# Residual taken from the gathered rows, one weight slot more, and a tail summed on two engines

## What is computed

```python
def _hier_moe(x, ...):                      # gate: for each token, weight of each expert, two are nonzero
    for g in range(N_EXPERT_GROUPS):
        hg = jnp.einsum('nd,edf->nef', x, w_gate[g])
        hu = jnp.einsum('nd,edf->nef', x, w_up[g])
        a = jax.nn.silu(hg) * hu * gate[:, g, :, None].astype(x.dtype)
        y = y + jnp.einsum('nef,efd->nd', a, w_down[g]).astype(jnp.float32)
...
h1 = layer_norm(DN_ALPHA * x + mix, ln1_g, ln1_b)
f = _hier_moe(h1, ...)
return layer_norm(DN_ALPHA * h1 + f, ln2_g, ln2_b)        # DN_ALPHA = 2 ** 0.25
```

## Time and profile before

| | |
|---|---|
| time, median of 3 runs | 1012.26 us (1011.37 to 1013.74) |
| profiled execution: its own time | 1013.08 us |
| profiled execution: span | 1011.3 us |
| PE busy | 906.9 us, 90% |
| DVE busy | 553.9 us, 55% |
| ACT busy | 410.1 us, 41% |
| POOL busy | 135.6 us, 13% |
| DMA, mean over the span | 270 GB/s |

### The profile page before, as it was taken

The page is one execution under the profiler, slowest core; times in us unless marked ns, Lnnn a source line. Parts: engine busy times, 40 slices in busy tenths (PEclk is TensorE's granted clock), DMA queues, the critical chain, the costliest instruction groups (busy, mean ns, idle before and its releaser), DMA issues.

```text
span 1011.3 us, 13331 instructions
## 1 busy us (share of the span) xinstructions
PE 906.9 (90%) x5132; PEld 644.8 (64%) x5132; DVE 553.9 (55%) x1023; ACT 410.1 (41%) x748; POOL 135.6 (13%) x83
## 2 busy tenths in 40 slices
PE   6999999986999999769999835999999999999684
PEld 6999879953555545437888524666666666656331
DVE  5202020049566665683554367676767676767248
ACT  5202020033564555471222122646465555546145
POOL 0000000140000000000000002254545321121100
PEclk9999999998999999988999955999999999999987
DMA  9999999198686666409722291899999999997293
GB/s 350 328 346 338 375 351 348 56 391 244 215 327 236 244 235 225 167 1 359 244 89 68 77 385 48 301 358 372 358 358 352 358 354 371 361 360 274 83 381 130
DMA packets 54847, 273.49 MB, mean 270 GB/s; under 512 B 13984, under 2 KB 16544, under 8 KB 39680
## 3 DMA queue, kind: packets, MB, share of 16 engines
q1 hardware_dynamic: 46016, 247.97, 67.8%
q0 software_dynamic: 8768, 24.66, 6.9%
HBM read 256.33 MB, written 95.30 MB: 348 GB/s over the span
## 4 chain that ended last, share of the span: by engine, by line
PE 77%; DVE 11%; DMA 5%; ACT 3%; issue 3%; SPq 0%; POOLq 0%; DVEq 0%; ACTq 0%
PE psum L636 69%; PE psum L695 4%; PE psum L874 2%; DMA back<-w_gu 2%; DMA front<-w_gu 2%; DVE back L1222 1%; DVE front L1232 1%; DVE front L1233 1%; DVE front L1579 1%; ACT back L490 1%; DVE stats L1207 1%; DVE back L1204 1%; PE psum L834 1%; ACT back L986 1%; DMA middle<-pair_d 1%
## 5 line engine op out<-in xcount | busy, mean ns | idle before, releaser
L636 PE MATMUL psum<-back,front 128*64 128x128 f32 (+1 forms) x896 | 148.6, 359 | 7.7 <-ACT back L490 4.4
L1645 POOL DMA_INDIRECT pair_d<-front,back x32 | 84.1, 2628 | 200.4 <-ACT front L1097 143.2
L636 PEld LDWEIGHTS psum<-back,front 128*64 128x64 f32 (+1 forms) x896 | 70.3, 148 | 62.9 <-issue 53.7
L636 PE MATMUL psum<-gu_high,xg_high 128*112 128x512 f32 x256 | 104.3, 407 | 2.1 <-DVE xg_low L1472 2.1
L636 PE MATMUL psum<-gu_high,xg_low 128*112 128x512 f32 x256 | 102.0, 399 | 0.0
L636 PE MATMUL psum<-x_high,w_high 128*128 128x352 f32 x288 | 94.2, 327 | 8.3 <-DVE w_low L361 8.3
L636 PE MATMUL psum<-gu_low,xg_high 128*112 128x512 f32 x256 | 101.5, 397 | 0.0
L636 PE MATMUL psum<-front 64*128 64x256 f32 (+5 forms) x384 | 91.5, 494 | 10.8 <-DVE stats L1204 10.1
L636 PE MATMUL psum<-x_low,w_high 128*128 128x352 f32 x288 | 93.5, 325 | 0.0
L636 PE MATMUL psum<-x_high,w_low 128*128 128x352 f32 x288 | 93.5, 325 | 0.0
L490 ACT COPY back<-psum 128x512 f32<-128x512 f32 (+1 forms) x88 | 46.9, 547 | 85.5 <-PE psum L695 85.3
(11 more groups left out here) (199 smaller groups left out, 1626.4 us busy)
## 6 DMA issues: line engine op xcount, KB each, us to landing
out_win_k_s<-cache_win_k SPq DMA_DIRECT2D x16, 2044.0 KB, 13.7
out_win_v_s<-cache_win_v SPq DMA_DIRECT2D x16, 2044.0 KB, 12.6
back<-w_down SPq DMA_DIRECT2D x24, 1024.0 KB, 14.3
front<-w_gu SPq DMA_DIRECT2D x22, 1024.0 KB, 11.9
middle<-w_gu SPq DMA_DIRECT2D x22, 1024.0 KB
back<-w_gu SPq DMA_DIRECT2D x20, 1024.0 KB, 14.4
back<-winkT SPq DMA_DIRECT2D x8, 1792.0 KB, 7.6
back<-cache_win_v SPq DMA_DIRECT2D x8, 1024.0 KB, 7.2
```

The source lines that it names most:

```text
L636: return nc.tensor.matmul(out, lhsT, rhs, start=start, stop=stop, skip_group_check=True)
L1645: G.indirect_dma_start(pair_d, bass.IndirectOffsetOnAxis(ap=IDX[0:CAP, NE + e:NE + e + 1], axis=0), YS[e % 2][0:CAP, :], None, bounds_chec ...
```

## The change

1. Residual. ALPHA * h1 is no longer added in the tail. Each token has two expert rows, and the whole sum is scaled by 2 / ALPHA: each expert's output row becomes (2 / ALPHA) * weight * down + h1, with h1 from the gathered rows in XG. Two such rows add up to (2 / ALPHA) * (ALPHA * h1 + f). The normalisation undoes the factor: the variance is scaled by ALPHA^2 / 4, and the gain ln2_g by ALPHA / 2. XG is therefore kept until the output is written, and has five buffers. The gather of expert e + 3 no longer waits for PE's transposes of expert e.
2. Who does what in the expert stage. DVE now makes both halves of the output (y_out, each a scalar_tensor_tensor of 112 x 512 from PSUM and XG). ACT gets active_out, ahead of silu.
3. Weights. There are four w_gu slots and five w_down slots; the new ones lie where H1 lay. The first loads now include w_gu of expert 3 and w_down of expert 4, behind a wait for the last transposes and stores of H1. Then the load for e waits for the products of e - 4.
4. Tail. Chunks 0, 4 and 8 are summed by DVE in SBUF (own_sum), the other six by PE. The separate pass L1579 is gone: ACT and the first DVE pass read the sum from PSUM or from YP.

The diff, without its overflow path and renamed counts:

```diff
-        GU_AT, GUH_AT = (0, 18576, 27024), (4096, 22672)
+        GU_AT, GUH_AT = (0, 18576, 27024, 37520), (4096, 22672)
...
-        WD = [at(x, 2, D) for x in (11264, 44688, 46736, 48784)]
-        XG = [at(x, D) for x in (31120, 32144, 50832)]
+        WD = [at(x, 2, D) for x in (11264, 44688, 46736, 48784, 41616)]
+        XG = [at(x, D) for x in (31120, 32144, 50832, 35472, 36496)]
...
+        PE_SUM = [c for c in range(CH) if c % 4]
+
+        def row_sum(c):
+
+            if c % 4 == 0:
+                return YP[c][:, 0, :]
+            j = PE_SUM.index(c)
+            return PS[:, 1024 * (j % 4):1024 * (j % 4) + 1024]
+
+        def summed(eng, c):
+
+            if c % 4:
+                eng.wait_ge(s_ysum, PE_SUM.index(c) + 1)
+            else:
+                eng.wait_ge(s_vsum, c // 4 + 1)
...
             load_dn(sp, 3)
-
-            for e in range(3, NE):
+            sp.wait_ge(s_ht, 2 * CH)
+            sp.wait_ge(s_h1d, 16 * CH)
+            for half in range(2):
+                load_gu(sp, 3, half)
+            load_dn(sp, 4)
+
+            for e in range(4, NE):
                 for half in range(2):
-                    sp.wait_ge(s_gu, 2 * (e - 3) + half + 1)
+                    sp.wait_ge(s_gu, 2 * (e - 4) + half + 1)
                     load_gu(sp, e, half)
-                if e >= 4:
-                    sp.wait_ge(s_y, e - 3)
+                if e >= 5:
+                    sp.wait_ge(s_y, e - 4)
                     load_dn(sp, e)
...
             def down(e):
                 pe.wait_ge(s_at, e + 1)
-                pe.wait_ge(s_wd[e % 4], 16 * (e // 4 + 1))
-                if e:
-                    pe.wait_ge(s_ya, e)
-                    pe.wait_ge(s_yd, e)
+                pe.wait_ge(s_wd[e % 5], 16 * (e // 5 + 1))
                 for n in range(2):
+                    if e:
+                        pe.wait_ge(s_yd, 2 * (e - 1) + n + 1)
                     for f in range(2):
...
-            for c in range(CH):
+            pe.wait_ge(s_yd, 2 * NE)
+            for j, c in enumerate(PE_SUM):
                 m = rows(c)
                 pe.wait_ge(s_yp[c], 16)
-                if c >= 4:
-                    pe.wait_ge(s_f1, c - 3)
+                if j >= 4:
+                    pe.wait_ge(s_f1, PE_SUM[j - 4] + 1)
...
-            def y_half(e):
-                act.wait_ge(s_y, e + 1)
+            def active_out(e):
+                act.wait_ge(s_tt, e + 1)
                 if e >= 2:
-                    act.wait_ge(s_ys[e % 2], 16 * (e // 2))
-                nc.scalar.activation(YS[e % 2][0:CAP, 0:512], bank(4)[0:CAP, :], ACT.Copy,
-                                     scale=GS[0:CAP, e:e + 1]).then_inc(s_ya, 1)
+                    act.wait_ge(s_y, e - 1)
+                nc.scalar.copy(AT[e % 2][:, :, 0:CAP], bank(6)[:, 0:2 * P].rearrange("p (a n) -> p a n", a=2)[:, :, 0:CAP]).then_inc(s_at, 1)
...
             for e in range(NE):
+                if e:
+                    active_out(e - 1)
                 silu(e)
                 if e + 1 < NE:
                     tokens_rounded(e + 1)
                 if e + 2 < NE:
                     weights_rounded(e + 2)
-                if e:
-                    y_half(e - 1)
-            y_half(NE - 1)
+            active_out(NE - 1)
...
-                r, mu, sq, std = RF[c][0:m, :], MV2[0:m, c, 0:1], MV2[0:m, c, 1:2], MV2[0:m, c, 2:3]
-                act.wait_ge(s_f1, c + 1)
+                r, mu, sq, std = row_sum(c)[0:m, :], MV2[0:m, c, 0:1], MV2[0:m, c, 1:2], MV2[0:m, c, 2:3]
+                summed(act, c)
...
-                nc.scalar.activation(std, sq, ACT.Sqrt, scale=1.0 / D, bias=EPSC[0:m, :]).then_inc(s_std2, 1)
+                nc.scalar.activation(std, sq, ACT.Sqrt, scale=ALPHA ** 2 / 4 / D, bias=EPSC[0:m, :]).then_inc(s_std2, 1)
...
-                step(V_.scalar_tensor_tensor(r, r, mu, GB2[0:m, 0, :], ALU.add, ALU.mult))
-                V_.scalar_tensor_tensor(r, r, std, GB2[0:m, 1, :], ALU.mult, ALU.add).then_inc(s_fo, 1)
+                V_.scalar_tensor_tensor(out, r, mu, GB2[0:m, 0, :], ALU.add, ALU.mult).then_inc(s_f1, 1)
+                dve.wait_ge(s_f1, c + 1)
+                V_.scalar_tensor_tensor(out, out, std, GB2[0:m, 1, :], ALU.mult, ALU.add).then_inc(s_fo, 1)
...
-            step(V_.tensor_tensor(v1, v1, p1, ALU.mult))
+            step(V_.scalar_tensor_tensor(v1, v1, 2.0 / ALPHA, p1, ALU.mult, ALU.mult))
...
-            def y_half(e):
+            def y_out(e):
                 dve.wait_ge(s_y, e + 1)
                 if e >= 2:
                     dve.wait_ge(s_ys[e % 2], 16 * (e // 2))
-                V_.tensor_scalar(YS[e % 2][0:CAP, 512:1024], bank(5)[0:CAP, :], GS[0:CAP, e:e + 1], None, ALU.mult).then_inc(s_yd, 1)
+                for n in range(2):
+                    h = slice(512 * n, 512 * n + 512)
+                    V_.scalar_tensor_tensor(YS[e % 2][0:CAP, h], bank(4 + n)[0:CAP, :], GS[0:CAP, e:e + 1], XG[e % 5][0:CAP, h],
+                                            ALU.mult, ALU.add).then_inc(s_yd, 1)
...
-            dve.wait_ge(s_y, NE)
+            dve.wait_ge(s_gb2, 32)
+            step(V_.tensor_scalar(GB2[:, 0, :], GB2[:, 0, :], ALPHA / 2, None, ALU.mult))
+
+            def own_sum(c):
+                dve.wait_ge(s_yp[c], 16)
+                y = YP[c][0:rows(c)]
+                V_.tensor_tensor(y[:, 0, :], y[:, 0, :], y[:, 1, :], ALU.add).then_inc(s_vsum, 1)
+
+            own_sum(0)
             for c in range(CH):
-                m = rows(c)
-                dve.wait_ge(s_ysum, c + 1)
-                V_.scalar_tensor_tensor(RF[c][0:m, :], H1[0:m, c, :], ALPHA, PS[0:m, 1024 * (c % 4):1024 * (c % 4) + 1024],
-                                        ALU.mult, ALU.add).then_inc(s_f1, 1)
-                if c:
-                    normalised(c - 1)
-            normalised(CH - 1)
+                if c % 4 == 3:
+                    own_sum(c + 1)
+                normalised(c)
...
             gather(1)
-            G.memset(XG[2], 0.0).then_inc(s_zero, 1)
+            for i in range(2, 5):
+                last = G.memset(XG[i], 0.0)
+            last.then_inc(s_zero, 1)
             await_(s_zero, 2)
             gather(2)
             for e in range(NE):
                 if e + 3 < NE:
-                    await_(s_tp, 2 * e + 2)
                     gather(e + 3)
                 if e:
-                    pool.wait_ge(s_ya, e)
-                    await_(s_yd, e)
+                    await_(s_yd, 2 * e)
                     scatter(e - 1)
```

More of the change, by code:

```diff
@@ L133, in build @@
         CATH, CATL = overlay("cat_high", 8448, KT, TOK), overlay("cat_low", 18576, KT, TOK)
-        GU_AT, GUH_AT = (0, 18576, 27024), (4096, 22672)
+        GU_AT, GUH_AT = (0, 18576, 27024, 37520), (4096, 22672)
         GUH = [overlay(f"gu_high{s}", GUH_AT[s], KT, 2 * DE) for s in range(2)]
-        GUL = [overlay(f"gu_low{s}", GU_AT[s], KT, 2 * DE) for s in range(3)]
+        GUL = [overlay(f"gu_low{s}", GU_AT[s], KT, 2 * DE) for s in range(4)]
         XGH = [overlay(f"xg_high{s}", (33168, 16896)[s], KT, CAP) for s in range(2)]
@@ L467, in load_gu @@
             k = slice(4 * half, 4 * half + 4)
-            sp.dma_start(GUF[e % 3][:, k, :], I["w_gu"][e][:, k, :]).then_inc(s_gf[e % 3][half], 16)
+            sp.dma_start(GUF[e % 4][:, k, :], I["w_gu"][e][:, k, :]).then_inc(s_gf[e % 4][half], 16)
         def load_dn(sp, e):
-            sp.dma_start(WD[e % 4], I["w_down"][e]).then_inc(s_wd[e % 4], 16)
+            sp.dma_start(WD[e % 5], I["w_down"][e]).then_inc(s_wd[e % 5], 16)
         R0 = 13600 + 324
@@ L1495, in _ @@
             for e in range(NE):
-                if e:
-                    active_out(e - 1)
                 if e >= 2:
-                    y_half(e - 2)
+                    y_out(e - 2)
                 if e + 1 < NE:
@@ L1504, in _ @@
                     tokens_rest(e + 1)
-            active_out(NE - 1)
-            y_half(NE - 2)
-            y_half(NE - 1)
+            y_out(NE - 2)
+            y_out(NE - 1)
             with overflow(dve):
```

63 lines of the change are left out of this document (26 added, 37 removed).

## The result

The changed kernel takes 999.29 us in the median of 4 runs (998.31 to 1000.77); the kernel before, beside it, 1011.82 us (4 runs, 1009.55 to 1013.74). The ratio is 0.9878 with a 95% interval of 0.9853 to 0.9904. The profiled execution took 1000.77 us, its span is 998.9 us against 1011.3: 12.4 us less, where the prediction's sum was 11.1 less. The medians differ by 12.5 us.

A forecast was written before the change was run, and what follows sets the result against it. PE, 77% of the chain, was taken to bound the kernel, with late w_gu transfers behind expert 21 and DVE in the tail. -3.96 + 0.15 - 7.3 = -11.1 us gave 1001.1 us from 1012.26; range 998.4 to 1006.5.

The forecast's parts named there:

- The beat to expert 31: Expert stage: with the fourth w_gu slot the 9.97 us beat holds to expert 31, at 936.06: -3.96 us.
- The lag: Expert stage: w_gu issue to landing grows 0.64 us per expert, to 22.5 us at the last load, 6 us inside.
- The early loads at nothing: Before the first gather: 3 MB more of loads fit the empty stretch, cost 0; uncovered, at most 8.9 us.
- The swap at nothing: Expert stage: DVE makes both output halves, ACT takes active_out; cost 0, since DVE has 2.9 us spare per expert.
- End of the stage: Last down starts about 0.55 us sooner, two DVE halves in a row add 0.7: sum +0.15 us.
- The tail: After chunk 0 lands (T0): DVE ends at T0 + 36.9 against T0 + 44.2 before, -7.3 us.
- PE's first sum: Tail, chunk 1: first 8 matmuls behind a long idle stretch take 6.12 us, later sums 3.43 each.
- The rival with a fast first sum: Tail: PE's first sum is not slow, chunks 1 to 3 come 2.7 us sooner: 998.4 us; chance 0.07.
- The stage that gains nothing: Expert stage: loads lag faster than 0.64 per expert or early loads issue late: 1005.1 us; chance 0.12.
- The tail that loses its overlap: Tail: ACT and DVE wait for each other, 0.4 us for each of 8 chunks: 1004.3 us; chance 0.10.
- The late scatter: Expert stage: DVE waits for the scatter two experts back, PE behind it; at 22.0 us landing, 1025 us; chance 0.03.
- PSUM as a source: Tail: the skill's rule makes six first DVE passes 0.4 us longer in all; the forecast took PSUM and SBUF as equal.

The follow-up runs named there:

- the one with fewer bytes: The changed kernel with three w_gu and four w_down slots, odd experts from 5 on loading 64 of 1024 w_down columns (output wrong): 1000.29 us.
- the late fill: The changed kernel with all slots, but the fourth w_gu slot first filled only when expert 0's products free PE: 1001.26 us.
- the kernel with the POOL sums: The changed kernel with the pair sums of chunks 4 and 8 on POOL instead of DVE: 1001.0 us.

## Why the prediction was right, term by term

- **The beat to expert 31.** Forecast 936.06 for its start, 936.01 came. That this agrees to 0.05 us is luck in part: it needs a stage that begins where before's did (626.3), and after's began at 626.5, where other traces have 623.9 to 626.8. The term of 3.96 us came out at 4.01 by this row and the earlier trace rows, 4.2 by the stage's length. The runs with three slots show that the w_gu slot earns it, the one with fewer bytes that lag is the cause, the late fill that the deadline is near 28.7 us.
- **The lag.** Forecast 22.5 us at the end, by 0.64 us per expert; it was 24.8. From 650 to 850 it grew by 18.0 us in 20 experts, 0.9 each, then levelled out. In the seven other kernels with four slots and the early loads, the last load took 22.8 to 24.5 us, so the forecast lies just below all eight. The straight line was loose: the margin was 3.9 us and not 6. Before's lag at 770, 13.2 us, is that of a single load; the four-slot kernels that fill early have medians of 13.9 to 16.0 there, the loads of the three-slot kernels took 13.3 to 15.0. No run explains the spread. From 840 on the late rounds of before also held its loads back.
- **The early loads at nothing.** They moved from before 606 to 619, and the first gather takes 4.25 us from issue to landing (4.18 before). Zero stands. Without the cover, filled late, they cost 0.8 us and not the 8.9 that bounded it, because they no longer stand ahead of the gather.
- **The swap at nothing.** Right with four slots, as the run with the copy back on DVE shows. Not with three, where ACT's order seems to cost about 1.5 us, by one trace on each side. The prediction asked only whether active_out would be in time in a steady beat; it did not ask what it waits behind when a load is late.
- **End of the stage.** From expert 31's start to the last scatter it is 15.85 us, before 15.67: +0.18, forecast +0.15. The last down starts after 0.74 us of waiting instead of 1.23, and the two halves of the output behind it take 1.41.
- **The tail.** Forecast T0 + 36.9, measured T0 + 35.7. The forecast times ran 1.0 to 1.2 us late from the first PE sum on: 8.8 against 7.8 for its end, 14.3 against 13.4 for DVE's end of chunk 1, 17.8 against 16.8, 21.7 against 20.7. Ahead of it they agree: chunk 0's add done at 1.4 (1.3), ACT's root at 5.4 (5.4), DVE's two passes at 8.3 (8.3). So one term was mis-sized, **PE's first sum: 6.12 us taken from before, 5.07 measured**. The eleven traces that begin it idle gave 5.1 to 6.7 us, in the median 6.3, and the six other traces in which the tail is that of after end it at T0 + 36.3 to 37.3. So 6.12 was a fair value, the forecast of T0 + 36.9 is what most traces of this tail show, and the trace of after drew a quick first sum. The rival with a fast first sum put it at 3.43, which none of them came near.
- **Rivals.** The stage that gains nothing: excluded by 309.53. The tail that loses its overlap: DVE waits 2.30 us for chunk 1 and 0.63 for chunk 2, behind PE's late first sum, and from there on no gap between its passes is over 0.1 us. The late scatter: the scatters did grow, from 9.8 to 11.9 us in the median, yet the maximum moved only from 12.9 to 13.1, and PE's waits for DVE L1501 are one of 0.7 us in all, the last down. The Trainium skill, DMA: Bandwidth & Descriptors, section Issuing engines are not separate DMA queues, has all issuers share the 16 engines. The traces show no effect of the length of the w_gu backlog on the scatter: from the end of its issue to its landing the scatter takes 7.5 us in the median of 640 to 730 and 7.3 of 820 to 920, while the w_gu loads go from 5 to 25. What made it longer is its issue on POOL, which counts from the same start: 4.55 us in after for all but the last three; in before 4.25 in the first half of the stage, where it landed in 10.2 to 12.9, and 0.96 in the late rounds, where it landed in 8.1 to 8.5. Counted from the end of the issue the median is 7.2 us in before and 7.4 in after. So the 8.1 us of the earlier trace rows, which the prediction held against this rival, belonged to a short issue and said less than it seemed; the rival failed all the same.
- **PSUM as a source.** By the Trainium skill, VectorE: DVE Perf Modes, section on the TRN2 errata, the tail would be 0.4 us longer (the prediction's estimate from its figures). Line 1245 runs from either memory in the same chunk loop, and the rows decide against it (ns min/median/max, first and last start):

```profile
L1245 DVE SCALAR_TENSOR_TENSOR front<-psum,stats,front x6: 1282/1282/1284, 971.7 to 991.1; 128x1024 f32<-128x1024 f32 x6
...
L1245 DVE SCALAR_TENSOR_TENSOR front<-middle,stats,front x1: 1285/1285/1285, 966.6 to 966.6; 128x1024 f32<-128x1024 f32 x1
```

The errors: 0.05 us too little gain in the stage, 0.03 too much at its end, 1.2 too little in the tail. They are all but 0.1 of the 1.3 us between -11.1 and -12.4. The forecast of the median, 1001.1, was missed by 1.8 us: 1.4 of it is the larger gain of the medians, 0.4 that the kernel before came out at 1011.82 instead of 1012.26. The profiled execution of after was the slowest of its four, and the other three have no trace, so what they saved on it, up to 2.5 us, stays open.

## What to carry to other kernels

When transfers run at their limit, an operand buffer is a deadline: read how issue to landing grows per step, and the step at which it meets the number of buffers times the beat is where the engine begins to wait. One slot more moves that point by a beat, and a slot that can be filled while the queues are empty costs nothing. A pass over a tile is worth its duration times the number of tiles only on the engine that bounds the loop; when it is gone, look for what the first tile waits for, since all others queue behind it. Before giving an idle engine a share, look at what it shares with the busy one.

## What the runs showed of the hardware

- **POOL and DVE hold each other up.** An add on POOL with its operands in SBUF stops a DVE pass with two SBUF operands until it ends (2.12, 3.19 and 3.26 us instead of 1.28), and one that reads PSUM not at all. The Trainium skill, SBUF — State Buffer, section SBUF: two separate sides, describes an exclusive lock on a port pair that GpSimd and a DVE operation with two SBUF inputs contend for; these three passes, each ending 1.08 us after the add, agree. POOL is held up as well: its add of 3.36 us at 978.24 instead of 2.35 began while a DVE pass with two SBUF operands ran. The same is seen the other way round in the expert stage: the scatter's issue on POOL takes 4.56 us when DVE's weight subtractions run, and 0.93 at the end of the stage, where they don't. In before it took 4.25 us in the rounds in which it met them and 0.96 from 832 us on, where it came behind them. Rows of after at 658 us:

```profile
658.35 4.62 DVE L1481 TENSOR_TENSOR gu_low<-front,gu_high 128x1024 fp32r<-128x1024 f32 x4
...
659.26 4.56 POOL L1659 DMA_INDIRECT pair_d<-front,back  x1 [4.12 <-DVE front L1501]
```

  The mean rose from 2.6 to 4.2 us: POOL now waits for DVE alone, and every scatter but the last three meets the subtractions. PE lost nothing by it.
- **The first product behind an idle stretch has no fixed price.** 5.1 to 6.7 us for the same eight matmuls; after (5.1) and the kernel with the POOL sums (6.7) differ in nothing ahead of them. It took 3.7 us when PE was kept busy. What differs is how long the granted clock stays at the lower level: in after it is 1.00 from 967 on, 3.4 us behind the first product, and in the POOL kernel it is still 0.50 from 967 to 969, 3.7 to 5.7 us behind its first product (963.28):

```profile
967.00:969.00 2.00, 2.00 (x4) 0.82 (x3) 1.76 (x2) 0.00 (x0) 0.00 (x0) 0.50 1.02 410
```

- **The lag is not only bandwidth.** At the same bytes per expert it ended between 22.8 and 24.8 us in kernels that differ only in the tail.
